# Two stacked transformer blocks on one core: weight parts of the recurrence in other places, both ends of the program rewritten

## What is computed

```python
def second_block(x, p, ...):
    for i in range(DEPTH_2):
        u = rms_norm(h, attn_norm_w[i])
        ...
        h = h + mixed @ w_out[i]
        h = h + gated_conv_ffn(rms_norm(h, ffn_norm_w[i]), ...)
        gate = jax.nn.sigmoid(rms_norm(h, ple_norm_w[i]) @ w_ple_gate[i])
        h = h + gate * (p[i] @ w_ple_proj[i])
    return rms_norm(h, final_norm_w)
```

```python
decay = exp(where(causal, cum[i] - cum[j], -inf))
scores = einsum('bhid,bhjd,bhijd->bhij', q, k, decay)
o = scores @ v + (q * exp(cum)) @ state
```

## Time and profile before

| | |
|---|---|
| median of 3 runs | 2384.47 us (2381.81 to 2384.67) |
| profiled execution | 2384.71 us, its span 2382.8 us |
| granted clock of TensorE, mean | 0.994 |
| instructions | 35317 |
| start, recurrence, end | 0 to 28, 211 to 354, 2329 to 2383 us of the span |

### The profile page before, as it was taken

The page is one execution under the profiler, slowest core; times in us unless marked ns, Lnnn a source line. Parts: engine busy times, 40 slices in busy tenths (PEclk is TensorE's granted clock), DMA queues, the critical chain, the costliest instruction groups (busy, mean ns, idle before and its releaser), DMA issues.

```text
span 2382.8 us, 35317 instructions
## 1 busy us (share of the span) xinstructions
PE 2336.5 (98%) x11510; PEld 1849.0 (78%) x11510; DVE 1098.9 (46%) x1880; ACT 865.1 (36%) x1357; POOL 1186.2 (50%) x1568
## 2 busy tenths in 40 slices
PE   8999999999999999999999999999999999999997
PEld 6776777677888888877678888888877688888885
DVE  5467665443323214526764344354346655242434
ACT  4355344454322223423333222245323243222254
POOL 5345554335564454544335646466533246555564
PEclk9999999999999999999999999999999999999998
DMA  4221112124232232243313323223333222323222
GB/s 159 89 89 50 50 45 67 54 63 133 88 115 89 96 106 82 96 137 98 111 51 100 106 85 104 93 78 107 106 115 98 80 89 97 106 88 106 84 93 89
DMA packets 67000, 219.93 MB, mean 92 GB/s; under 512 B 8128, under 2 KB 8512, under 8 KB 66896
## 3 DMA queue, kind: packets, MB, share of 16 engines
q1 hardware_dynamic: 57168, 196.21, 24.9%
q10 hardware_dynamic: 9728, 22.33, 3.0%
HBM read 212.18 MB, written 2.13 MB: 90 GB/s over the span
## 4 chain that ended last, share of the span: by engine, by line
issue 46%; POOL 39%; PE 9%; POOLq 2%; DVE 2%; ACT 1%; DMA 0%; DVEq 0%; ACTq 0%; SPq 0%
POOL w_lo L1854 38%; PE acc L284 2%; PE acc L286 2%; PE acc L285 2%; POOLq L1887 2%; PE sc L427 0%; PE pt L360 0%; PE po L378 0%; DMA x<-in_x 0%; DVE x L1827 0%; POOL qcur L1884 0%; ACT w_hi L734 0%; POOL kcur L1884 0%; POOLq L1851 0%; POOLq L1860 0%
## 5 line engine op out<-in xcount | busy, mean ns | idle before, releaser
L1854 POOL TENSOR_TENSOR w_lo<-raw,w_hi 128x256 fp32r<-128x256 f32 x1502 | 1138.6, 791 | 1167.5 <-ACT w_hi L734 1165.9
L284 PE MATMUL acc<-act_hi,w_hi 128*128 128x512 f32 x1768 | 706.9, 400 | 14.7 <-DVE act_lo L1222 10.5
L286 PE MATMUL acc<-act_hi,w_lo 128*128 128x512 f32 x1768 | 691.1, 391 | 0.0
L285 PE MATMUL acc<-act_lo,w_hi 128*128 128x512 f32 x1768 | 690.4, 390 | 0.0
L734 ACT CAST w_hi<-raw 128x1024 fp32r<-128x1024 f32 (+1 forms) x390 | 392.6, 1017 | 377.8 <-PE acc L286 221.2
L284 PE MATMUL acc<-y_hi,w_hi 128*128 128x512 f32 x1108 | 442.2, 399 | 0.9 <-POOL w_lo L1854 0.9
L286 PE MATMUL acc<-y_hi,w_lo 128*128 128x512 f32 x1108 | 433.4, 391 | 0.0
L285 PE MATMUL acc<-y_lo,w_hi 128*128 128x512 f32 x1108 | 432.8, 391 | 0.0
L284 PEld LDWEIGHTS acc<-act_hi,w_hi 128*128 128x128 f32 x1768 | 333.4, 189 | 92.5 <-issue 15.0
L286 PEld LDWEIGHTS acc<-act_hi,w_lo 128*128 128x128 f32 x1768 | 332.9, 188 | 71.2
L285 PEld LDWEIGHTS acc<-act_lo,w_hi 128*128 128x128 f32 x1768 | 333.4, 189 | 66.6 <-issue 1.9
(11 more groups left out here) (311 smaller groups left out, 2042.3 us busy)
## 6 DMA issues: line engine op xcount, KB each, us to landing
raw<-in_w_ffn_wide SPq DMA_DIRECT2D x120, 512.0 KB, 3.2
raw<-in_w_in SPq DMA_DIRECT2D x104, 512.0 KB, 3.3
raw<-in_w_rest SPq DMA_DIRECT2D x72, 512.0 KB, 3.2
raw<-in_w_gate SPq DMA_DIRECT2D x24, 512.0 KB, 3.3
raw<-in_w_ple_gate SPq DMA_DIRECT2D x16, 512.0 KB, 3.3
raw<-in_w_branch SPq DMA_DIRECT2D x24, 256.0 KB, 2.7
raw<-in_w_ffn_narrow SPq DMA_DIRECT2D x16, 384.0 KB, 3.0
...
```

Source lines behind the costliest of these rows:

```text
L284: nc.tensor.matmul(dst, w[0], src[0], start=start, stop=False)
L285: nc.tensor.matmul(dst, w[0], src[1], start=False, stop=False)
L286: return nc.tensor.matmul(dst, w[1], src[0], start=False, stop=stop)
L1854: last = nc.gpsimd.tensor_tensor(w_lo[:, slot, cut], raw[:, slot % 2, cut], w_hi[:, slot, cut], ALU.subtract)
```

## The change

**At the start** the eight `mix_g` gains and what lies ahead of them (12 columns) are loaded by themselves on ACT's queue, then x tiles 0 and 1; SP's queue has panel 0, x tile 2, panel 1, x tiles 3 to 7, the other parameters. ACT makes all eight high parts of x before the first square, DVE all eight low parts before the first sum; the low part of panel 0 is made in two halves. PE does four tiles of panel 0, four of panel 1, then the other four of both in turn, then one panel more before the sum of squares. **In the recurrence** POOL's pieces are dealt out by a table over levels 3 to 9 and levels 1 and 2 of the next pair, and ACT's second cast moves from level 3 to 4. `chunks_b(0)` moves from query tile 2 to 4, ahead of the last guest evacuation. **At the end** the two unused panels go; the sigmoid of panel j stands ahead of the copy and square of tile j - 1; panel 7 is evacuated ahead of the work on tile 6; squares 5 to 7 are summed by PE directly, one matmul each; tiles 6 and 7 are made from x in one step by DVE, which scales tiles 2 to 7, and POOL 0 and 1; SP and ACT store four tiles each. The helpers `norm_tile` of ACT and DVE are split in two (`norm_high` and `norm_square`, `norm_low` and `norm_add`), with the same instructions in them.

```diff
+GAINS = PARAMS["mix_g"][0] + KD
...
+    last_squares = [probs_t[:, 1, :], probs_t[:, 0, :], probs[:, 1, :]]
...
-            for j in range(2):
-                sp.dma_start(raw[:, j, :], dram["w_in1"][j]).then_inc(raw_loaded[j], 16)
-            for k in range(4, KD):
+            def load_x(k):
                 sp.dma_start(x[:, k, :], dram["x"][:, k, :]).then_inc(x_loaded[k], 16)
+
+            sp.dma_start(raw[:, 0, :], dram["w_in1"][0]).then_inc(raw_loaded[0], 16)
+            load_x(2)
+            sp.dma_start(raw[:, 1, :], dram["w_in1"][1]).then_inc(raw_loaded[1], 16)
+            for k in range(3, KD):
+                load_x(k)
+            sp.dma_start(params[:, GAINS:], dram["params"][:, GAINS:]).then_inc(S("param_loaded"), 16)
             sp.dma_start(consts[:, :, :], dram["consts"]).then_inc(S("const_loaded"), 16)
             sp.dma_start(masks[:, :, :], dram["masks"]).then_inc(S("const_loaded"), 16)
             sp.dma_start(positions[:, :], dram["positions"].partition_broadcast(P)).then_inc(S("pos_loaded"), 16)
...
-            load(dram["w_in1"][0:LOOK], 0, N_PANELS, LOOK)
-            sp.wait_ge(lo_done, N_PANELS + LOOK + 2)
+            sp.wait_ge(lo_done, N_PANELS + 2)
+            for ready, i, k in (("out_ready", 1, 2), ("out_ready", 3, 4), ("out_ready_too", 1, 0), ("out_ready", 5, 6)):
+                sp.wait_ge(S(ready), i)
+                sp.dma_start(out[k * P:(k + 1) * P, :], wb[:, k, :]).then_inc(S("out_stored"), 16)
...
-            normed_gemm(0, N_A, 12, 0)
+            def first_panel(j, k):
+                return tile_products(acc[:, j, :], j, 0, P, KD, act_in, part=range(k, k + 1))
+
+            pe.wait_ge(S("first_lo"), 1)
+            for k in range(4):
+                pe.wait_ge(S("norm_split"), k + 1)
+                first_panel(0, k)
+            pe.wait_ge(S("second_lo"), 1)
+            for k in range(4):
+                first_panel(1, k)
+            pe.wait_ge(lo_done, 4)
+            for k in range(4, KD):
+                pe.wait_ge(S("norm_split"), k + 1)
+                for j in range(2):
+                    last = first_panel(j, k)
+                    if k == KD - 1:
+                        last.then_inc(gemm_done, 1)
+            gemm(0, N_A + 2, 1, KD, act_in)
+            norm(0)
+            gemm(0, N_A + 3, 9, KD, act_in)
...
-            pe.wait_ge(S("norm_added", 2), 8 * KD + KD + 1)
+            pe.wait_ge(S("norm_added", 2), 2 + 8 * KD + 5)
             nc.tensor.matmul(sc[:, 0, :], c["ones"], probs[:, 0, :], start=True, stop=False)
-            pe.wait_ge(S("norm_sq"), 8 * KD + KD)
-            nc.tensor.matmul(sc[:, 0, :], c["ones"], probs_t[:, 1, :], start=False, stop=True).then_inc(S("norm_sum"), 1)
+            for k in (5, 6, 7):
+                pe.wait_ge(S("norm_sq"), 8 * KD + k + 1)
+                last = nc.tensor.matmul(sc[:, 0, :], c["ones"], last_squares[k - 5], start=False, stop=k == 7)
+            last.then_inc(S("norm_sum"), 1)
...
-            act.dma_start(params[:, :], dram["params"]).then_inc(S("param_loaded"), 16)
-            for k in range(4):
-                act.dma_start(x[:, k, :], dram["x"][:, k, :]).then_inc(x_loaded[k], 16)
+            act.dma_start(params[:, 0:GAINS], dram["params"][:, 0:GAINS]).then_inc(S("gain_loaded"), 16)
+            act.dma_start(x[:, 0, :], dram["x"][:, 0, :]).then_inc(x_loaded[0], 16)
+            act.dma_start(x[:, 1, :], dram["x"][:, 1, :]).then_inc(x_loaded[1], 16)
             act.wait_ge(started, 1)
...
-            act.wait_ge(S("param_loaded"), 16)
+            act.wait_ge(S("gain_loaded"), 16)
             for k in range(KD):
-                norm_tile(0, k, k % 2, "mix_g")
+                norm_high(0, k, "mix_g")
                 if k == 1:
                     high(0, 0, 1)
-            three_more(0, 0, N_A)
+            high(0, 0, 2)
+            for k in range(KD):
+                norm_square(0, k, k % 2)
+            for j in range(2):
+                high(0, 0, 3 + j)
+            act.wait_ge(S("param_loaded"), 16)
             norm_factor(0)
...
@@ -913,8 +956,8 @@
                         silus_b(PAIRS - 1)
                     if n == 2 and p:
                         gates_a(p - 1)
-                    if n in (2, 3, 6, 8):
-                        weights((2, 3, 6, 8).index(n))
+                    if n in (2, 4, 6, 8):
+                        weights((2, 4, 6, 8).index(n))
...
+                def last_norm(j):
+                    act.wait_ge(S("norm_x"), 8 * KD - KD + j + 1)
+                    settle(act)
+                    if j < 6:
+                        nc.scalar.activation(wb[:, j, :], x[:, j, :], ACT.Copy, scale=par("final_g", j)
+                                             ).then_inc(S("norm_hi"), 1)
+                    if j < KD - 1:
+                        act.wait_ge(S("norm_added", 2), 8 * KD + j + 1)
+                    square = probs_t[:, j % 2, :] if j < 5 else last_squares[j - 5]
+                    nc.scalar.activation(square, x[:, j, :], ACT.Square).then_inc(S("norm_sq"), 1)
+
                 for j in range(KD):
-                    if 0 < j < KD - 2:
+                    if 0 < j < KD - 2 and (l + 1 < LAYERS or LOOK + 2 + j < KD):
                         high(half, full, N_BLOCK1 + O_GATE + LOOK + 2 + j)
                     in_place(ACT.Sigmoid, "e_g", "e_gate", l * 8 + j, wb[:, j, :])
                     if j == KD - 1:
                         ln_exp_table()
                     if l + 1 < LAYERS:
                         norm_tile(l * 3 + 5, j, j % 2, "attn_w", l * KD + KD, attn_tiles(l + 1))
-                    else:
-                        norm_tile(l * 3 + 5, j, j % 2, "final_g", 0, (wb, None, 0))
+                    elif j:
+                        last_norm(j - 1)
                 if l + 1 < LAYERS:
                     three_more(half, full, N_BLOCK1 + PER_LAYER)
                     norm_factor(l * 3 + 5)
+                else:
+                    last_norm(KD - 1)
...
-            for k in (0, 1, 6, 2, 3, 7, 4, 5):
-                act.wait_ge(S("out_ready" if k < 6 else "out_ready_too"), k + 1 if k < 6 else k - 5)
+            for ready, i, k in (("out_ready", 2, 3), ("out_ready", 4, 5), ("out_ready_too", 2, 1), ("out_ready", 6, 7)):
+                act.wait_ge(S(ready), i)
                 act.dma_start(out[k * P:(k + 1) * P, :], wb[:, k, :]).then_inc(S("out_stored"), 16)
...
-            v.tensor_tensor(lower, lb, lb, ALU.subtract).then_inc(S("b_lb"), 1)
             norm_start()
             dve.wait_ge(hi_done, 1)
-            v.tensor_tensor(w_lo[:, 0, :], raw[:, 0, :], w_hi[:, 0, :], ALU.subtract).then_inc(S("first_lo"), 1)
             for k in range(KD):
-                norm_tile(0, k, k % 2, "mix_g")
+                if k < 2:
+                    cut = slice(k * 512, k * 512 + 512)
+                    v.tensor_tensor(w_lo[:, 0, cut], raw[:, 0, cut], w_hi[:, 0, cut],
+                                    ALU.subtract).then_inc(S("first_lo"), 1)
+                norm_low(0, k, "mix_g")
+            for k in range(KD):
+                norm_add(0, k, k % 2)
                 dve.drain()
+            dve.wait_ge(S("param_loaded"), 16)
+            v.tensor_tensor(lower, lb, lb, ALU.subtract).then_inc(S("b_lb"), 1)
...
                     if qt == 4:
                         dve.wait_ge(S("b_mixedlog"), p + 1)
                         v.tensor_tensor(z, z, tmp, ALU.add)
+                        if last:
+                            chunks_b(0)
                         guest(n + 3, (N_B + 3) % 4, wb[:, p + 4, :], "b_g")
                     if last and qt == 1:
                         scan_b(0, 2, 256)
                         scan_b(0, 1, 128)
                     if last and qt == 2:
                         key_256_b(0)
-                        chunks_b(0)
...
+                    if l + 1 == LAYERS and j == KD - 2:
+                        gate_panel(j + 1)
...
                         gate_panel(j + 1)
                     if l + 1 < LAYERS:
                         norm_tile(l * 3 + 5, j, j % 2, "attn_w", l * KD + KD, attn_tiles(l + 1))
-                    elif j < KD - 1:
-                        norm_tile(l * 3 + 5, j, j % 2, None)
-                    if j == KD - 2:
-                        gate_panel(j + 1)
+                        if j == KD - 2:
+                            gate_panel(j + 1)
+                    elif 0 < j < 6:
+                        norm_add(8, j - 1, (j - 1) % 2)
                 if l + 1 < LAYERS:
                     norm_end()
             dve.wait_ge(S("norm_rstd"), 9)
-            for k in range(6):
-                v.tensor_tensor(wb[:, k, :], wb[:, k, :], last_rstd, ALU.mult).then_inc(S("out_ready"), 1)
+            for k in range(2, KD):
+                if k < 6:
+                    last = v.tensor_tensor(wb[:, k, :], wb[:, k, :], last_rstd, ALU.mult)
+                else:
```

(40 more changed lines are left out.)

23 lines of the change are left out of this document (15 added, 8 removed).

## The result

The changed kernel takes 2358.46 us in the median of four runs (2358.27 to 2360.66), against 2383.31 (2381.81 to 2384.67) for the kernel before: ratio 0.9895, 95% interval 0.9884 to 0.9907, or 24.9 us less. The forecast was 2362.2 with a range of 2357 to 2370. The profiled execution took 2358.32 us with a span of 2356.26, so the two profiled executions are 26.4 us apart and their spans 26.5; the one of before took 2384.71, as long as the slowest of its four runs, and had two stretches at half clock in the recurrence.

A forecast was written before the change was run, and what follows sets the result against it. TensorE, busy 98% of the span, was taken as the bound, with only idle and low-clock time to win. Levels 7.2, clock 5.9, scan 0.9, start 5.0, end 3.5 sum to 22.5: 2384.7 to 2362.2 us, range 2357 to 2370.

The forecast's parts named there:

- Levels: Recurrence: dealing out GpSimd's weight pieces removes TensorE's 8.4 us of waits, less 1.2 charged; gain 7.2 us.
- tight level 6: Recurrence: TensorE reaches level 6 just as VectorE's chain ends; 0.3 us charged per pair, 1.2 in all.
- the new 1.1: Recurrence, level 1 of pair 0: a new TensorE wait of 1.1 us for the copy of the values, from the moved scan.
- named signs of being wrong: Waits at levels 7 to 9, a stretch at 0.5, or last logarithm over 8 us after the last product.
- The rival of GpSimd and VectorE in each other's way: Recurrence levels 7 to 9: pieces beside VectorE's work slow down; 2370 us, or 2376 with low stretches kept; chance 0.14.
- Clock: Recurrence: without waits of 1.4 to 1.6 us, both half-clock stretches go, 2.9 us each; gain 5.9.
- Scan: End of first attention: moving a scan removes a 2.0 us wait but adds one of 1.1; net gain 0.9 us.
- Start: First panels: first matmul at 8.0, pace doubling near 14.4, both panels done at 22.3; gain 5.0 us.
- The chain that I named as late next: Start: squares and adds to about 24, fourth panel's cast and low pieces to 27.6, needed at 28.4; holds barely.
- End: From TensorE's last product to the last logarithm: shorter chain for the last tiles; gain 3.5 us, bounds 2.5 and 4.7.
- I take 2369.3: End: chosen finish of tile 7's sum, between 2370.0 at low clock and 2368.1 at high; 3.5 us earlier.
- 10.05 us as before: Output stores, last sum to the end: two queues carry the same bytes, so the time stays 10.05 us.

The follow-up runs named there:

- one lump alone: Changed kernel with the third panel's four GpSimd pieces back in one block behind level 6, the second panel's two behind level 5: 2366.59 us.
- the dealing undone: Changed kernel with GpSimd's pieces again in blocks behind levels 1, 2, 4 and 6, and ScalarE's cast back at level 3: 2368.94 us.
- the scan back: Changed kernel with the copies and decays of the first chunk back at the third query tile of the last attention pair: 2360.99 us.

## Why the prediction was right

**Levels.** Right in mechanism, cautious in size. Forecast: 8.4 us of waits less 1.2 for a tight level 6, less the new 1.1: 6.1. Idle time of TensorE in the pairs fell by 6.9. The tight place cost 0.3 us in two pairs and nothing in the others. The run with one lump alone shows the cause, in two of its pairs: GpSimd's block in front of its next level. None of the named signs of being wrong appeared: TensorE's waits at the levels are at 1 and 6 alone and none at 7 to 9, no stretch is at 0.5, and the logarithm begins 6.5 us after the last product.

**The rival of GpSimd and VectorE in each other's way** had the contention right and its price wrong. It put the loss on the pieces; but these last 782 ns in pair 1 (776 before, 770 over all). VectorE pays. Two of its groups by line and shape (count, busy, mean ns, idle before), in pair 1 of the changed kernel:

```profile
L1504 DVE TENSOR_TENSOR x_queries<-kcur,wa 128x256 f32<-128x256 f32 x5 | 3.1, 623 | 1.3 <-ACT kcur L954 0.9 <-issue 0.2
L1473 DVE TENSOR_TENSOR_SCAN cums<-x,wb 128x128 f32<-128x128 f32 x4 | 2.6, 718 | 0.0
```

And in pair 1 with the dealing undone:

```profile
L1504 DVE TENSOR_TENSOR x_queries<-kcur,wa 128x256 f32<-128x256 f32 x5 | 2.6, 529 | 5.0 <-ACT kcur L954 4.8 <-issue 0.2
L1473 DVE TENSOR_TENSOR_SCAN cums<-x,wb 128x128 f32<-128x128 f32 x4 | 1.8, 525 | 0.0
```

VectorE is busy 1.5 to 1.6 us longer in that pair (26.44 against 24.98, and 24.84 before), and hides it in idle time: 26.4 of 32.1 us. These means are made of short and long ones. Of the four 128x128 scans in the pair, three took 0.70 to 0.90 us in the changed kernel and one with the dealing undone, the others 0.39 to 0.41; and none of these scans and query products (`x_queries`) that ran with GpSimd idle took over 0.43, in either kernel. The Trainium skill, page SBUF — State Buffer, section Who interferes with whom, has the second to issue block until the first is done. The longer scans agree in kind; by that rule I had let the pieces wait, and it is the rows that show which side does here.

**Clock.** Forecast 5.9 for two stretches. TensorE's busy time in pairs 1 and 2 is 3.2 and 3.3 us less than before, 6.5 together. The premise held, that the clock stays up without waits of that length at the levels: eleven traces have the pieces dealt out, with starts of the recurrence from 202.8 to 207.9, and none has a low stretch in any of the four pairs; the three with lumps (the kernel before, the dealing undone, one lump) have five. The new wait of 1.1 us at level 1 brought none. A wait of that length does not always bring one, though. In those three traces the three waits of 1.6 us were each followed by a low stretch, and of the five of 1.2 to 1.4 us two were; the 2.0 us ahead of the recurrence, in the kernel before and with the scan back, brought none.

**Scan.** Forecast: 2.0 gained, 1.1 lost, net 0.9. Measured 2.1 and 1.0 by the run that undoes it, net 1.1.

**Start.** Forecast 5.0, measured 5.40, and 4.5 in the comparison with the start undone. Two readings in it were off. The 14.4 should be 14.7 by its own terms (8.0, gaps of 0.65, 14 matmuls at 0.43), which is what its 22.3 for panel 2 is made of. And the 2.6 us without a gap ahead of the doubling before are 4.3, since the last gap there ended at 17.03. The first matmul came at 7.68 (8.0 forecast), the pace doubled at 13.9 (14.4), panel 2 began at 22.11 (22.3). The chain that I named as late next held as barely as said: VectorE's eighth add ended at 24.5, and GpSimd's pieces for the fourth panel,

```profile
24.72 5.61 POOL L1932 TENSOR_TENSOR w_lo<-raw,w_hi 128x256 fp32r<-128x256 f32 x8 [3.88 <-ACT w_hi L764]
```

four of the eight, were done near 27.5, half a microsecond before they are read. That agreement in tenths is partly luck, since the doubling alone scatters by 3.7 us. The Trainium skill, page TensorE: Matmul & The Clock Gate, section What's actually happening, says that how many matmuls run at half pace varies from run to run; the traces agree, with 9 to 17 of them in the ten with one start.

**End.** The mis-sized term: 3.5 forecast, 4.40 measured. The step that failed is "I take 2369.3", between sums at the low level and 2368.1 at the high one. Here the clock fell at 2348.6, after the sums, and not before them as in the kernel before (2366.2). Where it fell before the last sum, as in five of the variants, the interval is 7.47, a gain of 3.45. So the 3.5 was right for one of two cases, and I had given the other no chance of its own. Unseen was that one part, the evacuation moved ahead of tile 6, costs 0.6 us of the gain.

**Stores.** "10.05 us as before" was 0.63 off, for a reason that lies behind the last packet and stays open. That the two queues bring nothing was right.

Every term came out at its forecast or above, so the sum was cautious throughout, and not right by errors that cancel. The excess over the forecast is 0.8 of levels, 0.6 of clock and 0.3 in the busy time of pairs 0 and 3 (1.7 in the pairs), 0.9 of clock at the end, 0.6 behind the stores, 0.4 at the start and 0.4 in the two other intervals: 4.0 between 22.5 and 26.5. The medians are only 24.9 apart, since the profiled execution of before lies 1.4 us above its median and that of after at its own. Not tried: the dropped casts and pieces of the two dummy panels, GpSimd taking the first tiles and not the last at the end, and the parts of the start named above.
